# Stacked query halves for two kinds of attention scores, splits moved behind the evictions, one product per meta step

## The chip, the cores and the metric

The kernel runs on one core of a Trainium2 chip. A core has a matrix engine (PE, with its weight loads shown apart as PEld), a vector engine (DVE), a scalar engine (ACT), a general engine (POOL) and a queue processor (SP) that issues most of the DMAs. Each engine runs its own instructions in order; they wait for each other through semaphores. The metric is the device time of one launch in microseconds.

## The reference, cut to what matters

Two blocks in a row over 512 tokens of width 2048. The first has two layers. Each layer projects the normalised input, runs sliding-window attention (16 heads of 64, two groups of keys, a window of 128 tokens) and latent attention (8 heads, queries and keys of 128 plus a rotated part of 64 that all heads share on the key side), gates both and projects back:

```python
sc = (jnp.einsum('bqhd,bkhd->bhqk', qn, k_nope)
      + jnp.einsum('bqhd,bkd->bhqk', qr, k_r)).astype(jnp.float32) * scale   # latent
scores = jnp.einsum('bnqhgd,bnkhd->bnhgqk', qb, kk).astype(jnp.float32) * (SWA_HEAD_DIM ** -0.5)   # sliding
```

The second block has one layer, with 16 meta tokens ahead of the 512: a stick-breaking attention of 8 heads of 128, a pooling branch, a gated merge and an output projection.

```python
meta = jnp.broadcast_to(meta_tokens.astype(x.dtype)[None], (B, N_META, x.shape[2]))
hs = jnp.concatenate([meta, x], axis=1)
z = jnp.einsum('bqhd,bkhd->bhqk', q_blk.astype(jnp.float32), k_pre.astype(jnp.float32)) * (SB_HEAD_DIM ** -0.5)
```

## The kernel before, in words

Activations lie transposed: 128 channels on the partitions, 512 tokens along the row. Every fp32 operand is kept as two fp32r tiles, a high part (the value rounded) and a low part (what is left). A product takes three matmuls: high by high, high by low, low by high. The helper `three` issues them at lines 819, 820 and 821, so all products carry these three lines, and tiles and shapes tell them apart.

The work is a list of steps (`plan_steps`) that every engine walks in the same order, each issuing what is its own. The backbone are groups of up to four output tiles, one for each PSUM bank `bank0` to `bank3`. A group of 16 input tiles has eight chunks of two; a chunk is 24 matmuls (four outputs, two input tiles, three matmuls each). For each chunk SP loads raw weights, ACT rounds them into `w_hi` (L673, L675) once the chunk before has freed its place, and POOL subtracts to give `w_lo` (L808, L810). One output tile of one chunk is a slot. The function `later(gap, step)` puts side work so many slots on: the scores, transposes and value products of the heads run on PE between the backbone's matmuls.

Groups in order, for each of the two layers: cq, ckv, swa (four), gb (two), then mla0 and mla1 in turn (four pairs), wo (four). Then for the second block: sb (eight), pool (four), mix and up (eight pairs), wo (four). A swa group yields the queries and gates of four sliding heads, a pair mla0 and mla1 those of two latent heads, an sb group one stick-breaking head.

When the last chunk of a swa or sb group is through a bank, the step `read` has DVE copy the bank to SBUF with a factor (L1333), round it (CAST, L1114, in the helper `split`) and subtract (L1115), then signal `tile_ready`. The step `evac` behind the last product copies the banks that are left (L1216). The first head's scores of a swa group stand one slot behind the group's end (gap 1) and wait for `tile_ready` of the first query tile; its transposes stand five slots further. In a sliding head the scores contract over 64 partitions, since two heads share a query tile. In a latent head the 128 wide part and the 64 wide rotated part are two products into one bank, with a mask product (L1006) between them. DVE evaluates the rotation in `read_mla` (L1313, L1140, L1141, then `split`).

In sb and pool groups each chunk is followed by the step `meta`: for each input tile one matmul of 32 weight columns and 256 data columns against `w_hi` (L903) and one of 16 against `w_lo` (L905), both into `work0`. At the end `read_meta` copies it (L1344), and the step `meta_fold`, three slots on, waits for that copy (`meta_read`).

## Time and profile before

| | |
|---|---|
| median of 3 runs | 2930.22 us (2928.75 to 2932.04) |
| the profiled execution | 2928.94 us, span 2927.3 us |
| mean granted TensorE clock | 0.979 |
| PE busy | 2828.8 us, 97% of the span |
| DVE, POOL, ACT busy | 46%, 37%, 34% |
| sliding attention of layer 1, layer 2 | about 164 to 400 us, 908 to 1144 us |
| latent attention of layer 1, layer 2 | about 448 to 612 us, 1192 to 1356 us |
| stick-breaking groups | about 1530 to 2010 us |

PE is busy nearly all of the span, so it is read first: where it waits, and at what distance its matmuls start. A matmul's own duration (390 ns for 512 columns) contains pipeline depth; what one costs is the distance from its start to the next one's start (0.227 us for 512 columns). The other engines matter where PE waits for them. The stretches in the table are read from the first and last starts of the lines named above.

### The profile page before, as it was taken

Reading aid. Unit: us, or ns where it says so; the run is one execution under the profiler, and the core shown is the slowest. Engines: PE = TensorE matmul, PEld = TensorE weight load, DVE = VectorE, ACT = ScalarE, POOL = GpSimd, SP = SyncE. Lnnn points to the kernel's source line nnn. Section 1 sums busy time; section 2 is a strip of 40 time slices with the busy share of each in tenths; the row PEclk is TensorE's granted clock in tenths of the full one; section 3 lists DMA queues with packets and bytes.
Section 4 is the critical chain, followed back from the end, with each engine's and each line's share of the span. In section 5 each row is a group of like instructions: output and inputs, shape, how many; then the busy total and the mean of one; then the engine's idle time right before and its main releaser. Section 6 shows DMA issues by size and latency. Waiting matters only on the chain.

```text
span 2927.3 us, 33733 instructions
## 1 busy us (share of the span) xinstructions
PE 2828.8 (97%) x13276; PEld 2317.6 (79%) x13276; DVE 1344.8 (46%) x1855; ACT 997.3 (34%) x1558; POOL 1092.2 (37%) x536
## 2 busy tenths in 40 slices
PE   7999999999999999999999999999999999999995
PEld 5888887778888888777877788787878888888883
DVE  6646555732365565474345444444334222222345
ACT  5233434522323444442343233323223323233221
POOL 3443332234443333223443333333434444444441
PEclk9999998999999999899999999999999999999997
DMA  5332231234434222212442222222323333336332
GB/s 160 101 108 73 66 117 40 55 97 143 135 96 127 66 72 91 67 48 80 144 145 79 73 72 70 79 73 68 94 90 104 116 108 115 108 115 208 113 126 93
DMA packets 307613, 288.11 MB, mean 98 GB/s; under 512 B 33152, under 2 KB 256000, under 8 KB 306944
## 3 DMA queue, kind: packets, MB, share of 16 engines
q1 hardware_dynamic: 300656, 263.93, 30.3%
q10 hardware_dynamic: 6800, 22.02, 2.0%
q8 instruction: 106, 1.74, 0.2%
q14 instruction: 51, 0.42, 0.0%
HBM read 259.66 MB, written 26.21 MB: 98 GB/s over the span
## 4 chain that ended last, share of the span: by engine, by line
PE 81%; DVE 12%; ACT 4%; issue 1%; POOL 0%; DMA 0%; DVEq 0%; SPq 0%; ACTq 0%
PE bank L819 23%; PE bank L821 23%; PE bank L820 23%; PE work L819 2%; DVE probs L1545 2%; PE work L821 1%; PE work L820 1%; PE o_bank L819 1%; PE work L1040 1%; PE o_bank L820 1%; PE o_bank L821 1%; DVE pt L1553 1%; DVE mixed L1115 1%; DVE mixed L1114 1%; DVE probs L1122 1%
## 5 line engine op out<-in xcount | busy, mean ns | idle before, releaser
L810 POOL TENSOR_TENSOR w_lo<-w_raw,w_hi 128x1024 fp32r<-128x1024 f32 (+3 forms) x468 | 1003.5, 2146 | 1516.9 <-ACT w_hi L675 1516.9
L819 PE MATMUL bank<-act_in,w_hi 128*128 128x512 f32 x2664 | 1056.8, 397 | 27.6 <-DVEq L1204 13.7
L821 PE MATMUL bank<-act_in,w_lo 128*128 128x512 f32 x2664 | 1043.0, 392 | 0.0
L820 PE MATMUL bank<-act_in,w_hi 128*128 128x512 f32 x2664 | 1041.9, 391 | 0.0
L675 ACT ACTIVATE w_hi<-w_raw 128x1024 fp32r<-128x1024 f32 (+3 forms) x468 | 437.9, 937 | 1057.6 <-PE bank L821 632.9
L819 PEld LDWEIGHTS bank<-act_in,w_hi 128*128 128x128 f32 x2664 | 502.7, 189 | 135.6 <-POOL w_lo L810 18.8
L821 PEld LDWEIGHTS bank<-act_in,w_lo 128*128 128x128 f32 x2664 | 501.9, 188 | 108.0
L820 PEld LDWEIGHTS bank<-act_in,w_hi 128*128 128x128 f32 x2664 | 502.8, 189 | 99.4 <-issue 1.4
L819 PE MATMUL bank<-mixed,w_hi 128*128 128x512 f32 x768 | 300.3, 391 | 0.0
L820 PE MATMUL bank<-mixed,w_hi 128*128 128x512 f32 x768 | 299.4, 390 | 0.0
L821 PE MATMUL bank<-mixed,w_lo 128*128 128x512 f32 x768 | 299.3, 390 | 0.0
L1216 DVE TENSOR_TENSOR buf<-bank,r_x 128x512 f32<-128x512 f32 x84 | 57.0, 690 | 297.5 <-PE bank L821 294.9
L808 POOL TENSOR_TENSOR w_lo<-w_raw,w_hi 128x512 fp32r<-128x512 f32 x64 | 91.4, 1429 | 267.1 <-ACT w_hi L675 267.1
L819 PEld LDWEIGHTS bank<-mixed,w_hi 128*128 128x128 f32 x768 | 144.7, 188 | 30.0
L821 PEld LDWEIGHTS bank<-mixed,w_lo 128*128 128x128 f32 x768 | 144.6, 188 | 30.1
L820 PEld LDWEIGHTS bank<-mixed,w_hi 128*128 128x128 f32 x768 | 144.7, 188 | 29.7
L1181 DVE TENSOR_TENSOR buf<-bank,probs 128x512 f32<-128x512 f32 x48 | 33.2, 692 | 247.5 <-PE bank L821 247.5
L1553 DVE TENSOR_TENSOR pt<-work,pt 128x512 fp32r<-128x512 f32 (+2 forms) x136 | 76.6, 607 | 128.8 <-ACT pt L789 127.9
L759 ACT ACTIVATE probs<-probs,stat 128x256 f32<-128x256 f32 (+1 forms) x128 | 60.1, 471 | 140.3 <-DVE stat L1499 140.3
L673 ACT ACTIVATE w_hi<-w_raw 128x512 fp32r<-128x512 f32 x64 | 40.2, 628 | 150.6 <-PE bank L821 108.9
L1114 DVE CAST mixed<-buf 128x512 fp32r<-128x512 f32 x94 | 86.2, 917 | 4.8 <-DVE buf L1181 0.7
L1115 DVE TENSOR_TENSOR mixed<-buf,mixed 128x512 fp32r<-128x512 f32 x94 | 83.2, 885 | 3.2
(230 smaller groups left out, 2895.2 us busy)
## 6 DMA issues: line engine op xcount, KB each, us to landing
w_raw<-in_w_in SPq DMA_DIRECT2D x512, 128.0 KB, 2.4
w_raw<-in_w_in SPq DMA_DIRECT2D x224, 256.0 KB, 2.9
w_raw<-in_w_out SPq DMA_DIRECT2D x64, 512.0 KB, 3.6
w_raw<-in_w_in SPq DMA_DIRECT2D x32, 512.0 KB, 3.7
w_raw<-in_w_out SPq DMA_DIRECT2D x64, 256.0 KB, 4.6
probs<-in_xT SPq DMA_DIRECT2D x32, 256.0 KB, 4.4
x_scr<-buf ACTq DMA_DIRECT2D x32, 256.0 KB, 3.0
probs<-x_scr SPq DMA_DIRECT2D x32, 256.0 KB, 4.9
```

The lines of the kernel that those rows point to most:

```text
L675: act.activation(dst, src, ACT.Copy).then_inc(hi_ready, 1)
L759: act.activation(probs[:, at:at + w], probs[:, at:at + w], ACT.Exp, bias=stat[:, 1, i:i + 1], scale=SWA_SCALE, accum_out=stat[:, 2, i:i + 1])
L808: nc.gpsimd.tensor_tensor(lo[:, :, 0], raw[:, :, 0], hi[:, :, 0], ALU.subtract)
L810: nc.gpsimd.tensor_tensor(lo, raw, hi, ALU.subtract).then_inc(lo_ready, 1)
L819: pe.matmul(dst, lhs[0], rhs[0], start=start, stop=False, skip_group_check=skip)
L820: pe.matmul(dst, lhs[0], rhs[1], start=False, stop=False, skip_group_check=skip)
L821: return pe.matmul(dst, lhs[1], rhs[0], start=False, stop=stop, skip_group_check=skip)
L1114: link(v.tensor_copy(dst[:, 0], src))
L1115: return v.tensor_tensor(dst[:, 1], src, dst[:, 0].bitcast(F32), ALU.subtract)
L1216: v.tensor_tensor(dst, bank[m][:, :], r_x[:, :], ALU.mult).then_inc(bank_free, 1)
L1545: link(v.tensor_tensor_scan(back, back, back, 0.0, ALU.add, ALU.bypass))
L1553: v.tensor_tensor(pt[:, 1, lo:hi_], turn_bank(kind, b)[:, 0:hi_ - lo], pt[:, 0, lo:hi_].bitcast(F32), ALU.subtract).then_inc(pt_lo, 1)
```

## The change

1. Sliding scores. The query tile of two heads is split into two stacked tiles, one for each head: the high part on the head's own 64 partitions and the low part on the other 64. `k_swa` holds, for each of the two groups of keys, the high part on both halves, and the low part on the head's own half with zeros on the other. A score block is then two matmuls that contract over 128 partitions (L974, L975 of the kernel after) where it was three over 64.
2. Latent scores. The rotated query is stacked the same way (`qr_mla(e)`, one tile for each of the two heads, no longer doubled over pairs), and so is the rotated key (`kr_hi`, `kr_lo`). The latents that go through DRAM take 13 T instead of 12 T columns, and the fetch stands one chunk later.
3. Order. For swa and sb groups `read` only evicts. The splits are steps of their own behind the eviction of the fourth bank; `tile_ready`, the gate's signal and `read_meta` follow them.
4. Meta. `w_hi` and `w_lo` become one tile `w_split`; one matmul with 128 weight columns (32 of them meant) and 512 data columns (256 of each half) takes the place of L903 and L905. `read_meta` adds the two halves, which is one more DVE instruction.
5. The keys of the sliding heads are split in the step `swa_values`, and the sliding outputs pass through `sq` instead of `tmp`, which now holds the unsplit queries.

```diff
+        if kind in ("swa", "sb"):
+            steps += [("split", n, 0), ("split", n, 1)]
-                if kind == "gb" and i == 1 and c == 2:
+                if kind == "gb" and i == 1 and c == 3:
                     steps.append(("fetch_latents", l, a))
...
-                    x = meta_in[:, kt, :, :].rearrange("p s t -> p (s t)")
-                    pe.matmul(work[0][0:2 * META, 0:256], x, w_hi[:, c % RING, kk, cols],
-                              start=first and kk == 0, stop=False, skip_group_check=True)
-                    ins = pe.matmul(work[0][0:META, 0:256], x[:, 0:META], w_lo[:, c % RING, kk, cols],
-                                    start=False, stop=last and kk == 1, skip_group_check=True)
+                    x = meta_flat[:, 2 * META * kt:2 * META * kt + P]
+                    ins = pe.matmul(work[0][:, :], x, w_split[:, c % RING, :, kk, cols],
+                                    start=first and kk == 0, stop=last and kk == 1)
...
-                        q = mixed[rows, t, :, i * P:(i + 1) * P]
-                        k = k_swa[rows, :, k0:k0 + w]
-                        ins = three(dst, (q[:, 0], q[:, 1]), (k[:, 0], k[:, 1]), True, True)
+                        q = mixed[:, t, e, i * P:(i + 1) * P]
+                        pe.matmul(dst, q, k_swa[:, e, 0, k0:k0 + w], start=True, stop=False)
+                        ins = pe.matmul(dst, q, k_swa[:, e, 1, k0:k0 + w], start=False, stop=True)
...
-                            ins = three(dst, (qr[:, 0, blk], qr[:, 1, blk]), (kr[:, 0, 0:w], kr[:, 1, 0:w]),
-                                        False, True)
+                            pe.matmul(dst, qr_mla(e)[:, blk], kr_hi[:, 0:w], start=False, stop=False)
+                            ins = pe.matmul(dst, qr_mla(e)[:, blk], kr_lo[e][:, 0:w], start=False, stop=True)
...
-                    write_rotated(dst, swapped, c)
+                    rotate(swapped, c)
+
+                    for e in range(2):
+                        ins = v.tensor_copy(qr_mla(e)[ROPE * e:ROPE * e + ROPE, :], c[ROPE * e:ROPE * e + ROPE, :])
+                    link(ins)
+                    for e in range(2):
+                        own, other = slice(ROPE * e, ROPE * e + ROPE), slice(ROPE * (1 - e), ROPE * (1 - e) + ROPE)
+                        ins = v.tensor_tensor(qr_mla(e)[other, :], c[own, :], qr_mla(e)[own, :].bitcast(F32),
+                                              ALU.subtract)
+                    link(ins)
...
-                if m < 2:
-                    hi_lo = mixed[:, 2 * i + m] if kind == "swa" else (q_sb, k_sb[:, :, META:TM])[m]
-                    link(split(hi_lo, dst))
+
+            def split_tile(gi, m):
+
+                g = groups[gi]
+                kind, i = g["kind"], g["i"]
+                src = tmp[:, m, :]
+                if kind == "swa":
+                    q = mixed[:, 2 * i + m]
+                    for e in range(2):
+                        ins = v.tensor_copy(q[head_rows(e), e, :], src[head_rows(e), :])
+                    link(ins)
+                    for e in range(2):
+                        own, other = head_rows(e), head_rows(1 - e)
+                        ins = v.tensor_tensor(q[other, e, :], src[own, :], q[own, e, :].bitcast(F32), ALU.subtract)
+                    link(ins)
+                else:
+                    link(split((q_sb, k_sb[:, :, META:TM])[m], src))
                 signal(tile_ready)
+                if m == 1:
+
+                    signal(tile_ready)
+                    signal(tile_ready)
+                    signal(gate_in)
+                    if kind == "sb":
+                        read_meta(gi)
```

On DVE at the end of the second swa group of layer 1, before the change. `bank0` to `bank3` are the group's four outputs, `o_bank` is the output of the head before, `work0` and `work1` the scores of the group's first head.

```order
167 L1333 TENSOR_TENSOR buf<-bank0,r_x 128x512 [waits mm_done]
168 L1114 CAST mixed<-buf 128x512 [waits bank_free]
169 L1115 TENSOR_TENSOR mixed<-buf,mixed 128x512 [waits v_seq]
170 L1571 TENSOR_TENSOR buf<-o_bank,buf 128x512 [waits v_seq,pv_done]
171 L1114 CAST mixed<-buf 128x512 [waits v_seq]
172 L1115 TENSOR_TENSOR mixed<-buf,mixed 128x512 [waits v_seq]
173 L1333 TENSOR_TENSOR buf<-bank1,r_x 128x512 [waits v_seq,mm_done]
174 L1114 CAST mixed<-buf 128x512 [waits bank_free]
175 L1115 TENSOR_TENSOR mixed<-buf,mixed 128x512 [waits v_seq]
176 L1216 TENSOR_TENSOR buf<-bank2,r_x 128x512 [waits v_seq,mm_done]
177 L1216 TENSOR_TENSOR buf<-bank3,r_x 128x512 [waits mm_done]
178 L1488 SCALAR_TENSOR_TENSOR probs<-delta,work0 128x384 [waits bank_free,scored]
```

The same place after the change:

```order
181 L1346 TENSOR_TENSOR buf<-bank0,r_x 128x512 [waits mm_done]
182 L1622 TENSOR_TENSOR sq<-o_bank,buf 128x512 [waits pv_done,bank_free]
183 L1116 CAST mixed<-sq 128x512 [waits v_seq]
184 L1117 TENSOR_TENSOR mixed<-sq,mixed 128x512 [waits v_seq]
185 L1346 TENSOR_TENSOR buf<-bank1,r_x 128x512 [waits v_seq,mm_done]
186 L1220 TENSOR_TENSOR buf<-bank2,r_x 128x512 [waits mm_done,bank_free]
187 L1220 TENSOR_TENSOR buf<-bank3,r_x 128x512 [waits mm_done]
188 L1357 CAST mixed<-buf 64x512 [waits bank_free]
...
190 L1361 TENSOR_TENSOR mixed<-buf,mixed 64x512 [waits v_seq]
...
192 L1357 CAST mixed<-buf 64x512 [waits v_seq]
...
194 L1361 TENSOR_TENSOR mixed<-buf,mixed 64x512 [waits v_seq]
...
196 L1538 SCALAR_TENSOR_TENSOR probs<-delta,work0 128x384 [waits v_seq,scored]
```

The rounding and subtraction of the first query tile stood ahead of the evictions of the second to fourth bank; now both tiles' splits stand behind the fourth and ahead of the first read of the scores, with twice as many instructions, each over 64 partitions.

On PE at the same place, before: the last row of the group's last product, the next group's first product, the scores of the group's first head, and back to the backbone.

```order
882 L821 MATMUL bank3<-act_in,w_lo 128x512
883 L819 MATMUL bank0<-act_in,w_hi 128x512 [waits lo_ready,bank_free]
884 L820 MATMUL bank0<-act_in,w_hi 128x512
885 L821 MATMUL bank0<-act_in,w_lo 128x512
886 L819 MATMUL bank0<-act_in,w_hi 128x512
887 L820 MATMUL bank0<-act_in,w_hi 128x512
888 L821 MATMUL bank0<-act_in,w_lo 128x512
889 L819 MATMUL work0<-mixed 128x128 [waits v_ready,tile_ready,sum_read,pt_lo]
890 L820 MATMUL work0<-mixed 128x128
891 L821 MATMUL work0<-mixed 128x128
892 L819 MATMUL work0<-mixed 128x256
893 L820 MATMUL work0<-mixed 128x256
```

And after:

```order
866 L827 MATMUL bank3<-act_in,w_split 128x512
867 L825 MATMUL bank0<-act_in,w_split 128x512 [waits lo_ready,bank_free]
868 L826 MATMUL bank0<-act_in,w_split 128x512
869 L827 MATMUL bank0<-act_in,w_split 128x512
870 L825 MATMUL bank0<-act_in,w_split 128x512
871 L826 MATMUL bank0<-act_in,w_split 128x512
872 L827 MATMUL bank0<-act_in,w_split 128x512
873 L974 MATMUL work0<-mixed 128x128 [waits v_ready,tile_ready,sum_read,pt_lo]
874 L975 MATMUL work0<-mixed 128x128
875 L974 MATMUL work0<-mixed 128x256
876 L975 MATMUL work0<-mixed 128x256
```

The scores stand at the same distance behind the group's end, six matmuls, and wait for the same semaphores; a block has two rows where it had three.

On DVE at the end of the first sb group, before (`cos` is reused there as the place of the meta sums):

```order
1204 L1333 TENSOR_TENSOR buf<-bank0,r_x 128x512 [waits x_saved2,x_saved3,x_saved1,mm_done,x_saved0,v_seq]
1205 L1114 CAST mixed<-buf 128x512 [waits bank_free]
1206 L1115 TENSOR_TENSOR mixed<-buf,mixed 128x512 [waits v_seq]
1207 L1333 TENSOR_TENSOR buf<-bank1,r_x 128x512 [waits v_seq,mm_done]
1208 L1114 CAST mixed<-buf 128x512 [waits bank_free]
1209 L1115 TENSOR_TENSOR mixed<-buf,mixed 128x512 [waits v_seq]
1210 L1333 TENSOR_TENSOR buf<-bank2,r_x 128x512 [waits v_seq,mm_done]
1211 L1216 TENSOR_TENSOR buf<-bank3,r_x 128x512 [waits bank_free,mm_done]
1212 L1344 COPY cos<-work0 32x256 [waits bank_free,mm_done]
```

And after:

```order
1271 L1346 TENSOR_TENSOR buf<-bank0,r_x 128x512 [waits x_saved2,x_saved3,x_saved1,mm_done,x_saved0,v_seq]
1272 L1346 TENSOR_TENSOR buf<-bank1,r_x 128x512 [waits mm_done,bank_free]
1273 L1346 TENSOR_TENSOR buf<-bank2,r_x 128x512 [waits mm_done,bank_free]
1274 L1220 TENSOR_TENSOR buf<-bank3,r_x 128x512 [waits mm_done,bank_free]
1275 L1116 CAST mixed<-buf 128x512 [waits bank_free]
1276 L1117 TENSOR_TENSOR mixed<-buf,mixed 128x512 [waits v_seq]
1277 L1116 CAST mixed<-buf 128x512 [waits v_seq]
1278 L1117 TENSOR_TENSOR mixed<-buf,mixed 128x512 [waits v_seq]
1279 L1378 COPY cos<-work0 32x256 [waits v_seq,mm_done]
1280 L1379 TENSOR_TENSOR cos<-work0,cos 32x256 [waits v_seq]
```

The two splits have moved from between the evictions to between the fourth eviction and the read of the meta sums, and that read has an instruction more.

## Rows read from the trace of the kernel before

**Rows 1.** The page: each engine's busy time, its share of the span, its instructions.

```profile
PE 2828.8 (97%) x13276; PEld 2317.6 (79%) x13276; DVE 1344.8 (46%) x1855; ACT 997.3 (34%) x1558; POOL 1092.2 (37%) x536
```

**Rows 2.** PE's waits: line, releaser, us in total, times, longest.

```profile
PE work L819 <- DVE pt L1553: 16.4, 18, 2.4
```

**Rows 3.** PE in order of time, end of a swa group: start, duration, instruction.

```profile
222.84 0.39 PE L821 MATMUL bank<-act_in,w_lo 128*128 128x512 f32 x1
...
224.20 0.39 PE L821 MATMUL bank<-act_in,w_lo 128*128 128x512 f32 x1
224.52 0.32 PE L819 MATMUL work<-mixed 64*128 64x128 f32 x1
...
226.12 0.50 PE L819 MATMUL bank<-act_in,w_hi 128*128 128x512 f32 x1
226.45 0.40 PE L820 MATMUL bank<-act_in,w_hi 128*128 128x512 f32 x1
...
233.51 0.98 PE L1040 MATMUL work<-ident,probs 128*128 128x128 f32 x7 [0.27 <-DVEq L1204]
```

**Rows 4.** PE, an sb head's last score block, then one meta step.

```profile
1584.66 0.40 PE L997 MATMUL work<-mixed 128*128 128x512 f32 x1
...
1585.48 0.28 PE L903 MATMUL work<-w_hi,meta_in 128*32 128x256 f32 x1
...
1585.94 0.40 PE L819 MATMUL bank<-act_in,w_hi 128*128 128x512 f32 x1
```

**Rows 5.** PE, a latent head's scores, what follows, the transposes of the same head.

```profile
515.07 0.22 PE L819 MATMUL work<-act_in 128*128 128x128 f32 x1
...
520.54 0.50 PE L819 MATMUL o_bank<-pt,act_in 128*128 128x512 f32 x1
...
526.81 1.25 PE L1040 MATMUL work<-ident,probs 128*128 128x128 f32 x10
```

**Rows 6.** DVE in order of time, at the end of the swa group of rows 3.

```profile
219.27 1.66 DVE L1115 TENSOR_TENSOR mixed<-buf,mixed 128x512 fp32r<-128x512 f32 x1
...
223.83 0.43 DVE L1114 CAST mixed<-buf 128x512 fp32r<-128x512 f32 x1
224.30 0.69 DVE L1115 TENSOR_TENSOR mixed<-buf,mixed 128x512 fp32r<-128x512 f32 x1
...
226.76 0.55 DVE L1488 SCALAR_TENSOR_TENSOR probs<-delta,work 128x384 f32<-128x384 f32 x1 [0.33 <-DVE buf L1216]
```

**Rows 7.** POOL in order of time, the same place.

```profile
218.91 1.48 POOL L810 TENSOR_TENSOR w_lo<-w_raw,w_hi 128x512 fp32r<-128x512 f32 x1
224.56 1.58 POOL L808 TENSOR_TENSOR w_lo<-w_raw,w_hi 128x512 fp32r<-128x512 f32 x1 [4.17 <-ACT w_hi L675]
```

**Rows 8.** DVE in order of time, behind the scores of the latent head of rows 5.

```profile
521.44 0.17 DVE L1513 TENSOR_SCALAR stat<-stat 128x4 f32<-128x4 f32 x1
...
525.20 1.28 DVE L1519 TENSOR_SCALAR probs<-probs,stat 128x128 f32<-128x128 f32 x4
```

**Rows 9.** PE, the second sb group's last product and the meta fold behind it.

```profile
1626.42 0.39 PE L821 MATMUL bank<-act_in,w_lo 128*128 128x512 f32 x1
...
1631.34 0.39 PE L939 MATMUL o_bank<-fold,cos 32*128 32x16 f32 x2
```

**Rows 10.** DVE, the end of the same group.

```profile
1623.48 1.76 DVE L1114 CAST mixed<-buf 128x512 fp32r<-128x512 f32 x1
...
1629.98 0.41 DVE L1344 COPY cos<-work 32x256 f32<-32x256 f32 x1 [0.31 <-DVE buf L1216]
```

**Rows 11.** POOL, the same place.

```profile
1628.52 2.40 POOL L810 TENSOR_TENSOR w_lo<-w_raw,w_hi 128x1024 fp32r<-128x1024 f32 x1 [3.55 <-ACT w_hi L675]
```

**Rows 12.** PE, its first matmul after a wait in the latent attention of layer 1.

```profile
459.35 0.80 PE L819 MATMUL bank<-act_in,w_hi 128*128 128x512 f32 x1 [2.46 <-DVE act_in L1317]
```

**Rows 13.** Two stretches there: length, busy of five engines, PE's clock, DMA, GB/s.

```profile
480.00:500.00 20.00, 19.81 (x83) 16.05 (x83) 11.66 (x24) 8.58 (x21) 1.19 (x2) 0.67 0.08 23
500.00:520.00 20.00, 19.82 (x104) 16.02 (x105) 15.63 (x30) 11.73 (x27) 5.38 (x5) 1.00 0.16 42
```

More of the change, by code:

```diff
@@ L59 @@
 SB_COLS = 1344
+META_PAD = P - 2 * META
 OUT_ORDER = list(range(KT - 4, KT)) + list(range(KT - 4))
@@ L327, in hybrid_program @@
         stat = sb("stat", [P, 8, NB])
+        meta_acc = stat[:, :, :].rearrange("p a b -> p (a b)")[:, 0:META]
         bank = [ctx.enter_context(nc.psum_tensor(f"bank{i}", [P, T], F32)) for i in range(4)]
@@ L964, in _ @@
                     pe.wait_ge(tile_ready, tile("swa", h["l"], t // 2, t % 2) + 1)
-                    rows = slice(64 * e, 64 * e + 64)
                     for i in range(NB):
@@ L1133, in read_sum, with head_rows, rotate @@
                 inverse_root(dst, n)
+            def head_rows(e):
+                return slice(64 * e, 64 * e + 64)
             def full(gi, m):
                 v.wait_ge(mm_done, tile_done[gi, m])
-            def write_rotated(dst, swapped, c):
+            def rotate(swapped, c):
                 link(v.tensor_tensor(swapped, swapped, sin[:, :], ALU.mult))
                 link(v.tensor_tensor(c, c, swapped, ALU.add))
-                link(split(dst, c))
             def gate_answer():
@@ L1242, in evac @@
                     link(v.tensor_tensor(kr, kr, cos[:, :], ALU.mult))
-                    write_rotated(y_flat[:, 5 * 2 * T:6 * 2 * T].rearrange("p (s t) -> p s t", s=2),
-                                  swapped, kr)
+                    rotate(swapped, kr)
+                    v.memset(kr_new[ROPE:P, 1, :].bitcast(F32), 0.0)
+                    v.memset(kr_new[0:ROPE, 2, :].bitcast(F32), 0.0)
+                    link(v.tensor_copy(kr_new[:, 0, :], kr))
+                    for e in range(2):
+                        rows = slice(ROPE * e, ROPE * e + ROPE)
+                        ins = v.tensor_tensor(kr_new[rows, 1 + e, :], kr[rows, :],
+                                              kr_new[rows, 0, :].bitcast(F32), ALU.subtract)
+                    link(ins)
                 elif kind == "ckv":
@@ L1253, in evac @@
                     v.tensor_tensor(acc2[:, :], acc2[:, :], sq[:, :], ALU.add).then_inc(sum_in, 1)
-                    link(split(k_swa, tmp[:, 0, :]))
                 elif kind == "swa":
@@ L1343, in read_meta @@
                     v.wait_ge(folded, metas[0])
-                v.tensor_copy(meta_out[:, :], work[0][0:2 * META, 0:256]).then_inc(meta_read, 1)
+                link(v.tensor_copy(meta_out[:, :], work[0][0:2 * META, 0:256]))
+                v.tensor_tensor(meta_out[:, :], work[0][0:2 * META, 256:512], meta_out[:, :],
+                                ALU.add).then_inc(meta_read, 1)
                 metas[0] += 1
@@ L1391, in _ @@
                                          .to_broadcast([P, KT, META]), ALU.mult))
+                    link(v.memset(meta_flat[:, KT * 2 * META:].bitcast(F32), 0.0))
                     link(v.tensor_copy(meta_in[:, :, 0, :], work_m))
@@ L1399, in _ @@
                     read(*step[1:])
+                elif name == "split":
+                    split_tile(*step[1:])
                 elif name == "gate_min":
@@ L1458, in _ @@
                     v.wait_ge(lat_saved, 16 * (l + 1))
+                    k = tmp[:, 0, :]
+                    for e in range(2):
+                        own, other = head_rows(e), head_rows(1 - e)
+                        v.memset(k_swa[other, e, 1, :].bitcast(F32), 0.0)
+                        v.tensor_copy(k_swa[other, e, 0, :], k[own, :])
+                        ins = v.tensor_copy(k_swa[own, e, 0, :], k[own, :])
+                    link(ins)
+                    for e in range(2):
+                        own = head_rows(e)
+                        v.tensor_tensor(k_swa[own, e, 1, :], k[own, :], k_swa[own, e, 0, :].bitcast(F32),
+                                        ALU.subtract)
                     vts[0] += 1
@@ L1570, in _ @@
                         g_ = gate[:, t % 2 if kind == "swa" else 0, :]
-                    link(v.tensor_tensor(tmp[:, 0, :], o_bank[:, :], g_, ALU.mult))
-                    link(split(y, tmp[:, 0, :]))
+                    gated = sq[:, :] if kind == "swa" else tmp[:, 0, :]
+                    link(v.tensor_tensor(gated, o_bank[:, :], g_, ALU.mult))
+                    link(split(y, gated))
                     signal(y_done)
```

38 lines of the change are left out of this document (17 added, 21 removed).

## The prediction, from these rows

> **What bounds the kernel.** I read the page first, then PE's waits, then PE, DVE and POOL in order of time at the places that the change touches. PE is busy 97% of the span [rows 1], so what shortens PE's own work shortens the kernel unless a wait takes its place. PE's waits are few: the largest group, 16.4 us in 18 waits, stands in front of attention scores and is ended by DVE's last instruction of the head before [rows 2]. Waits for a bank to be evicted at the end of a swa or sb group are not in that view at all. So freeing banks earlier removes nothing, and what the moved splits now delay counts in full.
>
> **Sliding scores, the removed work.** A head's scores stand between two backbone matmuls. From the last of them before (224.20) to the second after (226.45) it takes 2.25 us [rows 3]; two backbone matmuls at 0.227 are 0.45 of it, the twelve score matmuls cost 1.80. That is more than twelve times 0.118, the distance of 256 column matmuls over 128 partitions (four between 1585.48 and 1585.94, [rows 4]), which would be 1.42: the change from 128 to 64 partitions and back costs the rest, about 0.2 at each side (0.32 from 224.20 to the first score, 0.33 from 226.12 to the next [rows 3]). With stacked halves there are eight matmuls over 128 partitions, 8 x 0.118 = 0.94. Saved: 0.86 for each of 32 heads.
>
> **Latent scores.** A head takes 5.47 us (515.07 to 520.54, [rows 5]), with two changes of partition count in each of its four blocks. Over 128 partitions throughout, an sb block of three 512 column matmuls and the mask product takes 0.82 (1584.66 to 1585.48, [rows 4]): 0.233 each and 0.12 for the mask. Five matmuls of each width (128 and 256 columns at 0.118, 384 at 0.175 between the two) and four masks are 5 x 0.644 + 0.48 = 3.70. Saved on PE: 1.8 for each of 16 heads, 29 us.
>
> The Trainium skill (TensorE: Matmul & The Clock Gate, Step-by-step: what each phase is for) says of the weight load that it scales with the columns and that "row count K doesn't matter here". By that only the dropped third counts: 0.46 a sliding head, 0.64 a latent one. The rows contradict it where the count changes between neighbours; it is a rival below.
>
> **Meta.** A step of four 256 column matmuls takes 0.46 (1585.48 to 1585.94, [rows 4]); two of 512 columns take 0.45. For 96 steps that is 0 to 1.5 us gained; I take 1.
>
> **The moved splits at the end of a swa group.** The group's last product ends at 223.23 (222.84 + 0.39, [rows 3]); call it 0. PE reaches the first head's scores at +1.2. Before, that tile had long been split. Now DVE evicts bank 3 (0.69, to about +0.75) and then splits: two CASTs and two subtractions over 64 partitions. Their row length is 512 as before, so I take the durations of the full ones: 0.43 and 0.69 when nothing is in the way [rows 6], in all +3.1 with the links. But POOL makes `w_lo` just then: its first instruction starts at 224.56, +1.3 [rows 7]. The subtraction at 219.27 took 1.66 instead of 0.69 because POOL's ran until 220.39 [rows 6, 7]: the two engines exclude each other there. With one POOL instruction (1.3) in the way the first tile is ready at +4.45, so PE waits 3.3 us; with none 1.9; with two 4.5. Behind the wait all of PE stands, the backbone too.
>
> The second tile's split (2.4 to 3.6 more) is in front of DVE's first read of the scores. That read now starts at about +8.1. Before it started at 226.76 and the transposes, which wait for the chain that it begins, at 233.51, 6.75 later [rows 3, 6]. So the transposes come at +14.8 instead of +10.3: 4.5 us lost per group with that head's saving already in it (between 1.9, with POOL never in the way, and 5). Three heads remain, 3 x 0.86 = 2.6 gained. Net +1.9 for each of 8 groups: +15 us, between -5 and +20.
>
> The Trainium skill (SBUF — State Buffer, SBUF: two separate sides) calls the shared port pair an exclusive lock, held for a whole instruction. If POOL takes it in every gap between DVE's instructions, that is two in the way, and the sum would be 8 x 1.2, some 10 us, higher.
>
> **Latent attention, what is given back.** DVE is nearly full there (15.63 of 20 us, [rows 13]). Behind the scores of rows 5 it finishes the maxima at about 521.6, then reads the next rotated query, and only then scales the probabilities, until 526.48 (525.20 + 1.28); PE transposes at 526.81 [rows 5, 8]. The rotated read grows by a CAST and a subtraction, 0.43 + 0.69 = 1.12. The maxima can end some 1.7 earlier, so the probabilities come 0.6 earlier, and PE gains 0.6, not 1.8. In the other head of a pair DVE's output work of the head before stands in front of the maxima, and I get 0.7. So 1.3 per pair, 10 us in 8 pairs; and where PE runs at half its clock it is later than DVE, so more of the saving comes through there: 3 more by estimate. I take -13; the ends are 0 (DVE's longer read eats all) and -29.
>
> **Sb groups.** The meta fold starts at 1631.34, and the copy that it waits for ended at 1630.39 (1629.98 + 0.41, [rows 9, 10]). The group's last product ends at 1626.81 [rows 9]. Now: bank 3 evicted at about 1627.5; CAST and subtraction of q until 1628.75; then POOL takes its turn, wanted at 1628.52, for 2.40 us [rows 11]. The CAST at 1623.48 shows what that does: 1.76 instead of 0.43 [rows 6, 10]. So the split of k runs from 1631.1 to 1632.3, and the two instructions of the meta sums (0.41 each and a link) until 1633.3. PE waits 2.0 us in each of 8 groups: +16, 0 if POOL comes behind k's split, +20 at most.
>
> **Hidden.** The keys' split in `swa_values` adds eight DVE instructions, some 4 us at 0.43 and 0.69 each, in the middle of a group, with PE's first use of the keys a slot behind the group's end; the fetch of the latents is issued one chunk later and still has four chunks of backbone (24 x 0.227 = 5.4 us each) over it; the split of the rotated key lengthens DVE by about 2 us at the start of ckv, under that group's backbone. Should a cover fail, each costs its own length at most, twice in the kernel. In pool groups the longer read of the meta sums (0.5) lies under the three slots before the fold. I put nothing for them.
>
> **Sum.** Against the profiled execution's 2928.94 us (span 2927.3; the median of the runs is 2930.22, 1.3 higher): +15 (sliding) - 13 (latent) - 1 (meta) + 16 (sb) = +17, so 2946 us.
>
> **Rivals.**
> 1. *The splits meet no POOL instruction, and the saved PE time comes through.* Sliding -5, sb 0, meta -1, latent between -13 and -29: 2910 to 2894, with latent -13 it is 2910. For it: DVE is in no way full in these places, and the two engines' order is decided by tenths. Against: POOL's start follows the chunk's end by about the same distance at every group end. It decides if the first tile is ready by +3.1.
> 2. *PE's clock falls.* After the wait of 2.46 us the matmul took 0.80 and not 0.39 [rows 12], and stretches of latent attention run at a granted clock of 0.67, a mixture of the full and the half level (2.4 and 1.2 GHz), against 1.00 [rows 13]. The sum has 8 new waits of 3.3 us and 8 of 2.0. A clock of 0.67 over 20 us loses 6.6 us of full clock; a quarter of that, 1.7 us, behind each of the 16 waits is +27: 2973. Against: a good part of it would lie in the time in which PE waits for the transposes anyway. It decides from waits of about 2.5 us.
> 3. *Only the number of matmuls counts, not the partitions.* Sliding saves 32 x 0.40 less (+13), latent some 8 less: 2967. Against it stand rows 3 to 5.
> 4. *The gain and the loss cancel*: half of the groups with POOL in the way gives about 2930.
>
> **Chances.** Forecast with its own spread (2935 to 2957) 0.45, rival 1 0.24, rival 2 0.15, rival 3 0.05, rival 4 0.11. Within 0.2% (5.9 us, about what a measurement can tell from no change) of 2930.2 lies rival 4 and little else: same 0.12; faster 0.25, slower 0.63. The range runs from rival 1 to rival 2: 2908 to 2974.
>
> **What would show it.** In the trace after: sliding score matmuls 0.118 apart with no longer distance at either side, a latent head's scores 3.7 us long; new waits of PE in front of the first scores of each swa group (about 3.3 us, 8 times) and in front of the meta fold (about 2, 8 times); longer waits for the transposes of latent heads. No waits at the group ends would prove the contention wrong, and a time under 2920 with it.

## The result, and the profile after

The changed kernel takes 2987.13 us (median of 4 runs, 2986.28 to 2995.32) against 2930.30 us before (4 runs): ratio 1.0199, 95% interval 1.0186 to 1.0212. It is slower, as forecast, but by 57 us and not by 16, and outside the range of 2908 to 2974. The profiled execution took 2986.28 us, its span 2984.6. The first row of the page after, beside [rows 1]:

```profile
PE 2823.3 (95%) x12892; PEld 2293.4 (77%) x12892; DVE 1413.8 (47%) x1934; ACT 996.0 (33%) x1558; POOL 1099.5 (37%) x536
```

PE issues 384 matmuls fewer, yet is busy for only 5.5 us less. Its waits after, the view of [rows 2] (line, releaser, us in total, times, longest):

```profile
PE work L974 <- DVEq L1208: 32.1, 8, 4.7
PE work L825 <- DVE pt L1603: 16.5, 12, 2.4
PE o_bank L943 <- DVE cos L1379: 16.2, 8, 2.0
```

The two new waits that the prediction named (the first and the third row) are there, each 8 times. The end of the swa group of [rows 3, 6, 7], PE first:

```profile
233.01 0.40 PE L827 MATMUL bank<-act_in,w_split 128*128 128x512 f32 x1
237.17 0.45 PE L974 MATMUL work<-mixed 128*128 128x128 f32 x1 [3.76 <-DVEq L1208]
...
239.01 0.63 PE L825 MATMUL bank<-act_in,w_split 128*128 128x512 f32 x1
239.44 0.63 PE L826 MATMUL bank<-act_in,w_split 128*128 128x512 f32 x1
...
240.54 0.39 PE L826 MATMUL bank<-act_in,w_split 128*128 128x512 f32 x1
240.77 0.39 PE L827 MATMUL bank<-act_in,w_split 128*128 128x512 f32 x1
```

DVE in the same stretch:

```profile
232.77 0.86 DVE L1357 CAST mixed<-buf 64x512 fp32r<-64x512 f32 x2
233.66 3.30 DVE L1361 TENSOR_TENSOR mixed<-buf,mixed 64x512 fp32r<-64x512 f32 x2
237.11 0.86 DVE L1357 CAST mixed<-buf 64x512 fp32r<-64x512 f32 x2
238.00 1.39 DVE L1361 TENSOR_TENSOR mixed<-buf,mixed 64x512 fp32r<-64x512 f32 x2
```

POOL in the same stretch:

```profile
233.33 1.41 POOL L814 TENSOR_TENSOR w_split<-w_raw,w_split 128x512 fp32r<-128x512 f32 x1 [4.44 <-ACT w_split L681]
234.71 1.71 POOL L816 TENSOR_TENSOR w_split<-w_raw,w_split 128x512 fp32r<-128x512 f32 x1
```

The two subtractions of the first tile take 3.30 us together, those of the second 1.39: POOL's two instructions lie in the first pair. Behind the wait of 3.76 us PE runs at its half level: backbone matmuls start 0.43 apart (239.01, 239.44) until 240.3 and then 0.23. The granted clock says it too, in a window of 7 us behind the wait and the next one (length, busy of PE, PEld, DVE, ACT, POOL, clock, DMA share, GB/s):

```profile
236.00:243.00 7.00, 5.83 (x23) 5.09 (x24) 5.80 (x10) 0.42 (x3) 0.41 (x1) 0.76 0.27 75
243.00:248.00 5.00, 5.00 (x27) 4.03 (x26) 1.59 (x4) 4.94 (x13) 2.14 (x2) 1.00 0.00 0
```

Latent scores, the first and the last side of a head as in [rows 5]: 3.76 us, not 5.47 (predicted 3.70).

```profile
497.75 0.33 PE L825 MATMUL work<-act_in 128*128 128x128 f32 x1 [2.17 <-DVE pt L1603]
...
501.51 0.40 PE L825 MATMUL o_bank<-pt,act_in 128*128 128x512 f32 x1
```

The latent attention of layer 1, 448 to 600 us, first in the kernel before and then after (columns as above):

```profile
448.00:600.00 152.00, 140.91 (x664) 113.12 (x663) 103.63 (x186) 72.27 (x167) 32.07 (x26) 0.87 0.17 45
```

```profile
448.00:600.00 152.00, 131.76 (x714) 111.05 (x713) 109.44 (x194) 73.83 (x170) 38.48 (x30) 0.98 0.24 71
```

PE waits more after, but its clock is 0.98 there and was 0.87. (The stage itself begins at 448 us before and at 467 after; over it alone the clock is 0.87 and 0.97.) The sb group's end of [rows 9 to 11], PE, DVE and POOL:

```profile
1643.62 0.39 PE L943 MATMUL o_bank<-fold,cos 32*128 32x16 f32 x2 [2.03 <-DVE cos L1379]
```

```profile
1639.08 2.40 DVE L1116 CAST mixed<-buf 128x512 fp32r<-128x512 f32 x1
1641.51 0.69 DVE L1117 TENSOR_TENSOR mixed<-buf,mixed 128x512 fp32r<-128x512 f32 x1
1642.71 0.41 DVE L1378 COPY cos<-work 32x256 f32<-32x256 f32 x1 [0.50 <-DVE mixed L1117]
```

```profile
1638.65 2.55 POOL L816 TENSOR_TENSOR w_split<-w_raw,w_split 128x1024 fp32r<-128x1024 f32 x1 [3.62 <-ACT w_split L681]
```

That is the forecast's picture: k's CAST takes 2.40 where q's took 0.43, and PE waits 2.03 (predicted 2.0).

All of this is small beside a thing that no step of the prediction had. In the stages behind attention PE never waits and runs at the full clock, and the instructions are the same. Still, in 200 us of them it does 885 matmuls before and 859 after (the number in brackets behind PE's busy time):

```profile
2600.00:2800.00 200.00, 200.00 (x885) 165.58 (x884) 52.36 (x58) 56.95 (x57) 88.88 (x37) 1.00 0.45 150
```

```profile
2600.00:2800.00 200.00, 200.00 (x859) 160.91 (x858) 48.99 (x50) 60.82 (x60) 87.05 (x36) 1.00 0.44 145
```

From the start times of the last 768 backbone matmuls: 226.7 ns apart before, 233.3 after, which is 6.7 ns more for each. The kernel has 10,296 of this shape.

### The profile page after: what moved, and what is told of

Its sections match the earlier page's. It is cut to its first block, busy times and chain, and to the rows that moved or that the text cites. A ratio compares the mean times of both kernels' runs of the same rounds, so it can differ in the third digit from the quotient of the medians.

```text
span 2984.6 us, 33082 instructions
## 1 busy us (share of the span) xinstructions
PE 2823.3 (95%) x12892; PEld 2293.4 (77%) x12892; DVE 1413.8 (47%) x1934; ACT 996.0 (33%) x1558; POOL 1099.5 (37%) x536
## 4 chain that ended last, share of the span: by engine, by line
PE 75%; DVE 17%; ACT 4%; issue 2%; POOL 1%; DMA 1%; SPq 0%; DVEq 0%; ACTq 0%
PE bank L825 22%; PE bank L826 22%; PE bank L827 22%; DVE probs L1595 2%; PE work L1042 1%; DVE mixed L1116 1%; DVE mixed L1361 1%; DVE pt L1603 1%; PE work L909 1%; PE o_bank L825 1%; PE o_bank L826 1%; PE o_bank L827 1%; DVE stat L1562 1%; DVE probs L1569 1%; DVE mixed L1117 1%
## 5 line engine op out<-in xcount | busy, mean ns | idle before, releaser
L816 POOL TENSOR_TENSOR w_split<-w_raw,w_split 128x1024 fp32r<-128x1024 f32 (+3 forms) x468 | 1009.8, 2160 | 1545.1 <-ACT w_split L681 1544.9
L825 PE MATMUL bank<-act_in,w_split 128*128 128x512 f32 x2664 | 1074.8, 403 | 32.6 <-DVEq L1208 13.6
L826 PE MATMUL bank<-act_in,w_split 128*128 128x512 f32 x2664 | 1059.9, 398 | 0.0
L827 PE MATMUL bank<-act_in,w_split 128*128 128x512 f32 x2664 | 1059.5, 398 | 0.0
L681 ACT ACTIVATE w_split<-w_raw 128x1024 fp32r<-128x1024 f32 (+3 forms) x468 | 437.9, 938 | 1091.0 <-PE bank L827 703.2
L825 PEld LDWEIGHTS bank<-act_in,w_split 128*128 128x128 f32 x2664 | 507.7, 191 | 154.6 <-POOL w_split L816 19.1
L827 PEld LDWEIGHTS bank<-act_in,w_split 128*128 128x128 f32 x2664 | 506.4, 190 | 121.2
L826 PEld LDWEIGHTS bank<-act_in,w_split 128*128 128x128 f32 x2664 | 507.6, 191 | 115.4 <-issue 1.4
L825 PE MATMUL bank<-mixed,w_split 128*128 128x512 f32 x768 | 303.7, 395 | 0.0
L826 PE MATMUL bank<-mixed,w_split 128*128 128x512 f32 x768 | 303.1, 395 | 0.0
L827 PE MATMUL bank<-mixed,w_split 128*128 128x512 f32 x768 | 303.1, 395 | 0.0
L814 POOL TENSOR_TENSOR w_split<-w_raw,w_split 128x512 fp32r<-128x512 f32 x64 | 92.2, 1441 | 288.7 <-ACT w_split L681 288.5
L827 PEld LDWEIGHTS bank<-mixed,w_split 128*128 128x128 f32 x768 | 144.5, 188 | 34.3
L825 PEld LDWEIGHTS bank<-mixed,w_split 128*128 128x128 f32 x768 | 144.5, 188 | 33.9
L826 PEld LDWEIGHTS bank<-mixed,w_split 128*128 128x128 f32 x768 | 144.5, 188 | 33.6
L679 ACT ACTIVATE w_split<-w_raw 128x512 fp32r<-128x512 f32 x64 | 40.1, 626 | 151.3 <-PE bank L827 116.6
L795 ACT ACTIVATE pt<-work 128x512 fp32r<-128x512 f32 (+2 forms) x136 | 64.4, 531 | 59.2 <-PE work L1042 59.2
L1442 DVE SCALAR_TENSOR_TENSOR probs<-buf,probs 128x1024 f32<-128x1024 f32 x20 | 45.7, 2325 | 65.6 <-ACT probs L661 65.6
```

The lines of the kernel that those rows point to most:

```text
L681: act.activation(dst, src, ACT.Copy).then_inc(hi_ready, 1)
L795: act.activation(pt[:, 0, lo:hi_], turn_bank(kind, b)[:, 0:hi_ - lo], ACT.Copy).then_inc(pt_hi, 1)
L814: nc.gpsimd.tensor_tensor(lo[:, :, 0], raw[:, :, 0], hi[:, :, 0], ALU.subtract)
L816: nc.gpsimd.tensor_tensor(lo, raw, hi, ALU.subtract).then_inc(lo_ready, 1)
L825: pe.matmul(dst, lhs[0], rhs[0], start=start, stop=False, skip_group_check=skip)
L826: pe.matmul(dst, lhs[0], rhs[1], start=False, stop=False, skip_group_check=skip)
```

## The experiments

Below, the "aligned change" is run 4, the changed kernel with its weight tiles moved 128 bytes further on. Times by stage, in us, are the distances between the same backbone matmuls in one trace of each kernel: start (from the first one to the end of the first swa group), swa, latent and sb groups, and the rest behind sb, in which nothing but the backbone bounds. The stages of layer 2 are cut 96 backbone matmuls (22 us) longer than those of layer 1, so they are compared down the columns only. Two traces with the same instructions and the same aligned operands, runs 2 and 4, differ by up to 2.6 us in a stage. Each ratio is that of the means, against runs of the kernel before made beside it.

| kernel | time, us | ratio to before (95%) | start | swa 1, 2 | latent 1, 2 | sb | rest |
|---|---|---|---|---|---|---|---|
| before | 2930.3 | 1 | 149.6 | 241.6, 263.3 | 152.7, 179.9 | 514.1 | 831.2 |
| after | 2987.1 | 1.0199 (1.0186–1.0212) | 153.9 | 254.9, 278.2 | 133.9, 161.4 | 542.2 | 852.9 |
| 1 before, weights +384 B | 2975.2 | 1.0147 (1.0131–1.0162) | 152.7 | 243.7, 265.6 | 152.8, 180.5 | 517.0 | 852.7 |
| 2 after, weights +0 | 2956.6 | 1.0085 (1.0069–1.0102) | 150.6 | 253.8, 276.5 | 133.7, 164.5 | 545.2 | 830.6 |
| 3 before, later tiles +384 | 2930.1 | 0.9997 (0.9986–1.0009) | 150.0 | 242.8, 263.7 | 151.3, 179.9 | 514.1 | 831.4 |
| 4 aligned change (+512) | 2953.3 | 1.0072 (1.0057–1.0087) | 152.2 | 254.0, 276.0 | 134.8, 166.6 | 542.6 | 830.3 |
| 5 all splits back | 2918.5 | 0.9962 (0.9947–0.9976) | 151.7 | 250.9, 274.2 | 139.6, 166.7 | 512.1 | 830.3 |
| 6 swa splits back | 2951.0 | 1.0071 (1.0056–1.0086) | 152.3 | 253.5, 273.2 | 133.8, 167.0 | 544.4 | 830.3 |
| 7 before, act_in +384 B | 2975.8 | 1.0149 (1.0125–1.0173) | 152.6 | 244.1, 265.5 | 149.9, 184.4 | 517.5 | 852.7 |
| 8 two products | 2922.9 | 0.9962 (0.9950–0.9975) | 150.6 | 237.6, 259.3 | 154.4, 180.0 | 513.9 | 831.1 |
| 9 latent and meta only | 2894.9 | 0.9879 (0.9866–0.9893) | 150.7 | 241.7, 264.7 | 135.0, 162.1 | 512.4 | 830.3 |
| 10 second split in a gap | 2878.6 | 0.9831 (0.9817–0.9844) | 151.5 | 233.2, 255.6 | 134.1, 168.1 | 512.9 | 830.3 |
| 11 before, weights +256 B | 2928.9 | 0.9987 (0.9977–0.9997) | 150.8 | 241.9, 264.6 | 152.8, 178.6 | 513.8 | 831.1 |
| 12 before, weights +64 B | 2976.1 | 1.0158 (1.0140–1.0177) | 153.3 | 244.1, 266.0 | 154.5, 179.0 | 518.0 | 852.9 |

**The layout, runs 1 to 4, 7, 11 and 12.** The change pads `meta_in` with 96 columns, 384 bytes. Everything allocated behind it moves by as much, `w_raw` and the tiles of both halves of the weights among it. The theory was that this place alone costs the 6.7 ns. Run 1 is the kernel before with

```diff
+        spare = sb("spare", [P, 96])
         w_raw = sb("w_raw", [P, RAW, 2, T])
...
-        meta_acc = sb("meta_acc", [P, META])
+        meta_acc = stat[:, :, :].rearrange("p a b -> p (a b)")[:, 0:META]
```

> The kernel before with 96 unused columns (384 bytes) between meta_in and the weight tiles, as the change puts them there; the instructions are the same (meta_acc lies in stat, as in the changed kernel, to make room). Theory A (the place of the weight tiles in SBUF costs each backbone matmul 6.7 ns): the distance of backbone matmuls goes from 0.2267 to 0.2333 us and the time up by 55 to 70 us, to 2985 to 3000. Theory B (the interleaved w_split tile costs it): no change, 2930. Theory C (something that the changed instructions do, such as more DVE traffic): no change, 2930.

Run 2 allocates the changed kernel's `meta_flat` behind all others:

> The changed kernel with meta_in and its pad allocated last, so that the weight tiles start at a multiple of 2048 bytes again; the instructions are the same. Theory A (place of the weight tiles): backbone matmuls 0.2267 apart again, time 2987 - 60 = 2920 to 2930. Theories B (interleaved tile) and C (other traffic): 0.2333 apart, 2987.

Run 3 has the spare columns of run 1 behind `w_lo`:

> The kernel before with the 96 unused columns behind w_lo: the weight tiles stay where they were, pt and all tiles behind it move by 384 bytes. Theory A, with the weight tiles as what counts: no change, 2930 (within 0.2%). If what counts is the place of the tiles behind (pt, probs, buf, r_x), it takes 55 to 70 us longer, as the first run.

Run 4:

```diff
         meta_flat = sb("meta_in", [P, KT * 2 * META + META_PAD], F32R)
+        r_meta = sb("r_meta", [P, META])
+        fold = sb("fold", [2 * META, META])
         w_raw = sb("w_raw", [P, RAW, 2, T])
```

> The changed kernel with r_meta and fold (64 bytes each) between meta_in and w_raw, so that the weight tiles are shifted by 512 bytes instead of 384 against the kernel before. Theory A in the form that rows of weights (128 columns of 4 bytes, 512 bytes) have to start at a multiple of 512: 0.2267 apart, 2920 to 2930. If a multiple of 2048 is needed: 0.2333 apart, 2987. Theories B and C: 2987.

The rest behind sb takes 852.7 in run 1 and 830.3 to 831.4 in runs 2 to 4, against 831.2 before. So it is the place of the weight tiles, in either kernel, that costs the longer distance; neither the interleaved tile (runs 2 and 4 have it) nor the tiles behind (run 3). The window of before's rows above, in run 1:

```profile
2600.00:2800.00 200.00, 200.00 (x858) 160.96 (x858) 49.54 (x52) 60.92 (x60) 86.98 (x36) 1.00 0.44 146
```

The whole time moved less than the theory had it (55 to 70 us): by 44 us in run 1 and by 31 and 34 us in runs 2 and 4, so all three times lie outside what was expected. In the latent stages and the sb groups of run 1 hardly anything of the longer distance arrives (0.1, 0.6 and 2.9 us). In the latent stages, where DVE is nearly full [rows 13], that can be DVE's pace; it was not tried. In the sb groups 1728 matmuls would give 11.5 us; where the other 9 went I have not settled. Run 7 shifts the other operand:

```diff
+        spare = sb("spare", [P, 96])
         act_in = sb("act_in", [P, KT, 2, T], F32R)
...
+        r_meta = sb("r_meta", [P, META])
+        fold = sb("fold", [2 * META, META])
         w_raw = sb("w_raw", [P, RAW, 2, T])
```

> The kernel before with act_in and mixed (the moving operand and the queries) shifted by 384 bytes and the weight tiles at a multiple of 512 (96 unused columns ahead of act_in; r_meta and fold, 128 bytes, between meta_in and w_raw). Theory (only the weights' rows count, they are what the engine loads as the stationary operand): no change, 2930, backbone 0.2267 apart. Rival (either operand counts): 2970 to 2980, as with the weights shifted.

My theory that only the stationary operand counts fell: with the activations off and the weights on a multiple of 512, the backbone matmuls are 233.3 ns apart again.

```profile
2600.00:2800.00 200.00, 200.00 (x858) 160.88 (x857) 49.75 (x51) 61.19 (x60) 86.16 (x36) 1.00 0.44 148
```

Runs 11 and 12 are run 1 with 64 and with 16 spare columns:

> The kernel before with the weight tiles shifted by 256 bytes. Theory A1 (any start that is no multiple of 512 bytes costs the same): backbone 0.2333 apart, 2970 to 2980. A2 (a multiple of 256 is enough): 0.2267, 2930. A3 (the cost grows with the distance from a multiple): between.

> The kernel before with the weight tiles shifted by 64 bytes. A1: backbone 0.2333 apart, 2970 to 2980. A2 (some power of two from 64 upwards is enough): 64 is no multiple of 128 or 256, so 0.2333; 0.2267 and 2930 would say that a multiple of 64 is enough, and then the 384 bytes would have had to be free as well.

Shifts of 256 and 512 bytes are free, those of 64 and 384 (a multiple of 128, but not of 256) cost the same. So moving the weights by a multiple of 256 bytes is harmless, and by one of 128 it need not be. Two things stay open. The traces hold no addresses, so all shifts are counted from the places in the kernel before. And each slow kernel moved one operand of the backbone against the other; none moved both alike. Whether each tile needs its place, or only the two against each other, was not tried. The same window in run 11, then in run 12:

```profile
2600.00:2800.00 200.00, 200.00 (x884) 165.62 (x884) 51.74 (x57) 56.95 (x57) 87.97 (x37) 1.00 0.45 150
```

```profile
2600.00:2800.00 200.00, 200.00 (x859) 160.28 (x858) 49.69 (x51) 61.13 (x60) 85.14 (x36) 1.00 0.44 148
```

**The moved splits, runs 5 and 6.** Both start from the aligned change. Run 5:

```diff
-        if kind in ("swa", "sb"):
-            steps += [("split", n, 0), ("split", n, 1)]
...
                 v.tensor_tensor(dst, bank[m][:, :], r_x[:, :], ALU.mult).then_inc(bank_free, 1)
                 v.wait_ge(bank_free, tile_no[gi, m] + 1)
+                if m < 2 and kind in ('swa', 'sb'):
+                    split_tile(gi, m)
```

> The changed kernel with the weight tiles shifted by 512 bytes (as the run before), and all splits done right behind the eviction of their bank again, as in the kernel before; stacked scores and the one meta product stay. Theory (moved splits cost their waits and the clock behind them, stacked scores save 0.86 us per sliding head): the waits in front of the sliding scores (32.8 us) and of the meta fold (16.9 us) go, the swa groups take 241.6 - 13.8 and 263.3 - 13.8 us, the sb groups about 514; in all 2870 to 2880. Rival 3 (only the number of matmuls counts, 0.40 to 0.46 a sliding head): 2884 to 2890. Rival (the gain of the stacked form is eaten by DVE's four instead of two split instructions): about 2900.

Run 6 does so for the swa groups alone:

> As the one above, but only the swa groups' splits are back behind their evictions; the sb groups' splits and meta sums stay behind the four evictions. Theory: swa as above, sb 542 us as in the changed kernel with its fold wait of 2.0 us in 8 groups; 2898 to 2908, about 29 above the one with all splits back.

Both kernels missed their forecasts (2870 to 2880 and 2898 to 2908) by about 40 us. In sb the undone move gives 30 us back, as expected. In the sliding stages it gives 3.1 and 1.9 us in run 5, 0.5 and 2.9 in run 6, where I expected 26 each. PE's waits of run 5 show why:

```profile
PE bank L823 <- DVE buf L1218: 24.1, 8, 3.3
```

And DVE there, at the same group's end as above:

```profile
229.12 0.69 DVE L1350 TENSOR_TENSOR buf<-bank,r_x 128x512 f32<-128x512 f32 x1
229.85 2.58 DVE L1365 CAST mixed<-buf 64x512 fp32r<-64x512 f32 x2
232.46 1.39 DVE L1369 TENSOR_TENSOR mixed<-buf,mixed 64x512 fp32r<-64x512 f32 x2
234.00 1.29 DVE L1218 TENSOR_TENSOR buf<-bank,r_x 128x512 f32<-128x512 f32 x2
```

The stacked form needs four instructions of 64 partitions for a tile, and each takes as long as one of 128 (0.43 and 0.69). With POOL's in the way, 4.0 us stand ahead of the evictions of banks 2 and 3, where [rows 6] have 1.15, and PE waits 3.0 for a bank. Behind the evictions the same work makes it wait 4.1 for the scores (32.8 us in 8, run 4). So the loss comes from the longer split, in either of these two places. PE's clock is part of it: in the two sliding stages 50 backbone distances are at the half level (0.43) in run 4 and 60 in run 5, none in the kernel before.

**The scores' own price, run 8.** The kernel before with

```diff
-                        ins = three(dst, (q[:, 0], q[:, 1]), (k[:, 0], k[:, 1]), True, True)
+                        pe.matmul(dst, q[:, 0], k[:, 0], start=True, stop=False)
+                        ins = pe.matmul(dst, q[:, 0], k[:, 1], start=False, stop=True)
```

> The kernel before without the third product (low half of the queries by high half of the keys) of the sliding scores: 8 matmuls over 64 partitions instead of 12, everything else unchanged. It leaves out that part of the scores. Theory (0.118 for each matmul, and 0.2 at each change between 128 and 64 partitions): 0.46 us saved for each of 32 heads, 15 us, so 2916; the step from and to the backbone stays 0.32 and 0.33. Rival 3 (the count alone): the stacked form saves no more per head than this does, 0.40 to 0.46.

From the last backbone matmul before a head's scores to the second behind them, without a wait, it takes 2.14 us before, 1.67 here and 1.28 with the stacked form (the first heads of the groups 2.25, 1.80 and 1.39). The first head of [rows 3], in this run:

```profile
223.70 0.39 PE L821 MATMUL bank<-act_in,w_lo 128*128 128x512 f32 x1
224.02 0.32 PE L972 MATMUL work<-mixed 64*128 64x128 f32 x1
...
224.95 0.28 PE L973 MATMUL work<-mixed 64*128 64x256 f32 x1
225.16 0.50 PE L819 MATMUL bank<-act_in,w_hi 128*128 128x512 f32 x1
225.50 0.39 PE L820 MATMUL bank<-act_in,w_hi 128*128 128x512 f32 x1
```

So the third product is worth 0.47, and the partitions 0.39 more: the distances on the two sides go from 0.32 and 0.21 to 0.23 and 0.12, and the one behind them from 0.34 to 0.24. But of the 15 us only 8 arrived in the sliding stages. The first head's transposes wait 0.75 for DVE in place of 0.27, and other heads wait for `pt`.

**Versions that are faster, runs 9 and 10.** Run 9 is run 5 with the sliding scores and their splits as in the kernel before:

> Only two of the change's parts: stacked halves for the latent scores, and the one 512 column product per meta step, with the weight tiles shifted by 512 bytes. Sliding scores with three products over 64 partitions and their two split instructions, and the sb splits, are as in the kernel before. Theory (the stacked sliding form costs more in DVE's four split instructions at a group's end than it saves on PE; latent and meta are pure gain): the swa groups take 241.6 and 263.3 us as before, so 9.3 + 10.9 less than in the run with all splits back: 2895 to 2902. Rival (sliding's stacked form is no loss, the 20 us come from the layout): swa stays at 251 and 274, 2918.

Run 10 is run 5 with the second tile's split in the first head's softmax, where DVE waits for ScalarE:

```diff
+        late_split = sem("late_split")
...
                     pe.wait_ge(tile_ready, tile("swa", h["l"], t // 2, t % 2) + 1)
+                    if t % 2:
+                        pe.wait_ge(late_split, 4 * h["l"] + t // 2 + 1)
...
                     ask(v.tensor_scalar(stat[:, 1, :], stat[:, 0, :], sinks8[:, l, no:no + 1], -SWA_SCALE,
                                         ALU.max, ALU.mult))
+                    if h["h"] % 2 == 0 and h["e"] == 0:
+                        split_tile(group_at["swa", l, h["h"] // 2], 1)
                     answer()
```

> As the run with all splits back, but the second tile's four split instructions of a swa group are issued where DVE waits 2.2 us for ScalarE's exponentials in the first head (its tile is evicted to acc, a semaphore of its own releases the scores of heads 2 and 3). Theory (what the stacked sliding form costs is DVE's time ahead of the evictions, 2.3 us and more for each tile): PE's waits for the banks (24.1 us in 8) go nearly all, swa groups about 241.6 - 13.8 and 263.3 - 13.8 us, in all 2865 to 2880. Rival (the splits collide with POOL wherever they stand, and the transposes come late in their place): 2895 to 2918.

Both times came out as expected (run 9 at the lower end, run 10 at the upper), and run 9's sliding stages too; those of run 10 are 5 and 6 us longer than its theory had them. DVE of run 10 at the group's end, with the split in the gap between lines 1555 and 1560:

```profile
223.75 1.29 DVE L1221 TENSOR_TENSOR buf<-bank,r_x 128x512 f32<-128x512 f32 x2
...
227.87 0.23 DVE L1555 TENSOR_SCALAR stat<-stat,sinks 128x4 f32<-128x4 f32 x1
228.00 0.85 DVE L1370 CAST mixed<-acc 64x512 fp32r<-64x512 f32 x2
228.89 1.39 DVE L1374 TENSOR_TENSOR mixed<-acc,mixed 64x512 fp32r<-64x512 f32 x2
230.43 0.16 DVE L1560 TENSOR_TENSOR stat<-stat 128x4 f32<-128x4 f32 x1
```

The bank waits are gone, and so are the distances at the half level. Against run 5 that is 18 us in each sliding stage, of which the bank waits are 12 and those distances about 6. The sliding stages are 8.5 and 9.1 us shorter than in run 9: of the 27 us that PE saves there (32 x 0.86), 18 arrive. Most of the rest is back in waits: in front of the transposes PE waits 19.7 us for DVE in run 10 and 12.5 in run 9. It is the fastest kernel here, 1.7% under the one before.

## Why the prediction was wrong

It missed because a term was missing. Without it the time would have come near the forecast (the aligned change took 2953.3 us against 2946), but that is luck: the terms of the sum are off by +10 (sliding), -18 (latent), +13 (sb with meta) and +3 us (start), and these nearly cancel. Point by point, by the aligned change's stages against those of before:

- **The missing term: +34 us** (2987.1 less 2953.3). The sum priced instructions and waits. It took the backbone's distance as a constant of the kernel and never asked what the new pad does to the addresses behind it. The diff shows the pad. The rows hardly show its price: in the kernel before, the keys of the sb scores do start 64 bytes (the 16 meta columns) into their tile, and the prediction read 0.233 a matmul from their block [rows 4] without asking why it is not 0.227; no run shows that the place is the reason there. The step that failed is the one in which a backbone matmul costs "0.227" after the change as before it, in the scores and in the covers alike, and in which the stages behind attention do not occur. The runs showed 0.233 in its place.
- **Sliding scores: right.** 0.86 a head was forecast, 0.86 came. Rival 3 is refuted: 0.39 of it is not the count of the products but the partitions (run 8). What was not in the sum is that a third of the gain goes back into waits for DVE (27 us on PE, 18 in run 10).
- **Splits of the swa groups: the mechanism right, the size short.** PE waits 3.76 to 4.71, 4.0 in the mean, not 3.3; POOL is in the way twice, for which the prediction had 4.5. The two subtractions took 3.30 against 1.39, and each ended some 0.5 behind one of POOL's two instructions. The trace agrees with the rule on the shared port (the Trainium skill, SBUF — State Buffer, SBUF: two separate sides), an exclusive lock that is held for a whole instruction. The swa stages lost 12.4 and 12.8 us, 3.1 a group instead of 1.9; the 50 distances at the half level, 10 us, are in that and were not in the sum. The blame was misplaced, though. I charged it to the move, and run 6 shows that the stacked split costs as much unmoved.
- **Latent attention: right in sign, -31 us instead of -13.** The scores shrank as forecast (3.76). What was mis-sized, as I read the rows, is what PE's clock gives back. I gave it 3 us in all. The clock rose from 0.87 to 0.96 in layer 1's stage and from 0.89 to 0.93 in layer 2's, and among the kernels with the new latent scores the stage goes with it: in layer 1 133.9 us at 0.97 (after) and 139.6 at 0.91 (run 5), in layer 2 161.4 at 0.98 (after) and 168.1 at 0.92 (run 10). There about two thirds of the full clock that is lost (the length times what the clock lacks) shows as time. By that, an estimate from one trace each, the clock is some 15 of the 31 us, and the work the rest. No run tested the clock by itself. Why it rose stays open: PE waits more there than before, 20 us in layer 1's stage against 11, so fewer waits are not the reason.
- **The sb groups: the wait right, the stage not.** 2.03 us against 2.0 (2.1 in run 4), but the groups lost 28 us and not 15. Of the 11 us beside the waits the greater part is rival 2's: behind the waits backbone matmuls start 0.43 apart, 33 times in run 4's sb groups, 36 in run 6's, once in run 5's and never before, so about 7 us.
- **Rival 2 was no rival but a part.** In the sliding stages and the sb groups together the kernel before has no backbone distance at the half level, the changed kernel 63 and the aligned change 83. That is 13 to 17 us for 16 new waits, 0.8 to 1.0 a wait. The granted clock itself (0.96 to 0.98 in these stages, 1.00 before) lost about 27 us of full clock in the changed kernel, which is the 1.7 a wait of the rival; part of it lies where PE waits or does the scores. Rivals 1 and 4 fell with the waits, which stood at every one of the 16 places.
- **Meta: about right**, -1.2 to -2.0 us in the sb groups (runs 5, 9 and 10) and -0.9 in the stages behind.
- **Hidden: not quite.** The start took 2.7 us more, though only 1.0 in run 2, which has the same instructions. What PE waits for there was not tried.

These add up: +25.2 - 31.3 + 28.4 + 2.7, and 0.2 for the stages between and behind, make 25, the difference of run 4's span and that of before; with the layout (32 between the spans of run 4 and the changed kernel) it is the 57 us.

## What to carry to other kernels

Read a diff for what it does to addresses too: a pad of a few bytes ahead of the operands can cost more than the instructions that it saves (here 384 bytes, 32 us, for a product that saved 2 to 3). Move operand tiles by multiples of 256 bytes, which was free in every run here, and test a suspicion of this kind first, by moving one allocation. And cost a new data layout by the instructions that produce it, at the place where the producer has no time to spare; on DVE, halves of the partitions cost here as much as all of them. Such work belongs into a gap in which that engine waits for another.

## What the hardware showed that I had not expected

- Backbone matmuls (128 x 128 stationary, 512 columns, 4 byte elements) start 226.7 ns apart with the tiles placed as before or the weights moved by 256 or 512 bytes, and 233.3 with the weights moved by 64 or 384 bytes, or the activations by 384. That is 16 cycles of 2.4 GHz in 544, the same for each of the three shifts. The pool products on `pt`, both of whose operands moved with the pad, are 230 ns apart in the kernels before and after, 227 in run 4 and 232 in run 3, where `pt` alone moved; they do not follow the rule of the backbone closely.
- Behind each of the eight waits of 3.8 to 4.7 us in the changed kernel 3 to 9 backbone matmuls started 0.43 apart; behind the eight of 2.0 us it was none in four cases and 3 to 7 in the others. So work that removed waits gained twice: the sliding stages of run 10, with run 5's instructions and without its bank waits, had a clock of 1.00 in place of 0.97.
- A DVE instruction on 64 partitions took as long as on 128: 0.43 the CAST, 0.69 the subtraction.
